# Moving a few waits: splits, loads and sums placed elsewhere in a one-core fp32 decoder layer on Trainium2

## The reference: what is computed

```python
h = rms_norm(x, norm_mix)
proj = h @ w_in + b_in                       # q, k, v of both head groups, gates
o_a = nsa_attention(...)                     # 16 heads: compressed, selected, window branch
o_b = swa_sink_attention(...)                # 16 heads: window of 128, a sink per head
x = x + concatenate([o_a, o_b]) @ w_out      # 2048 x 2048
h = rms_norm(x, norm_ffn)
x = x + (silu(h @ w_gate) * (h @ w_up)) @ w_down     # 2048 -> 5632 -> 2048
return rms_norm(x, norm_final)
```

## Time and profile before

| | value |
|---|---|
| median of three runs | 2010.52 us |
| the profiled execution: its own time | 2010.52 us |
| its span, first to last instruction | 2008.6 us |
| mean granted TensorE clock | 0.999 of full speed |
| PE busy | 1986.3 us (99%) |
| DVE busy | 1635.1 us (81%) |
| ACT busy | 986.1 us (49%) |
| DMA, mean over the span | 153 GB/s |

### The profile page before, as it was taken

One profiled execution on the slowest core, in us unless ns is written; L12 is line 12 of the kernel. 1 busy time (PEld: TensorE's weight loads), 2 busy tenths in 40 slices (PEclk: granted clock), 3 DMA queues, 4 the chain that ended last, 5 costly groups with the idle time before them and its releaser, 6 DMA issues.

```text
span 2008.6 us, 33101 instructions
## 1 busy us (share of the span) xinstructions
PE 1986.3 (99%) x13573; PEld 1793.7 (89%) x13573; DVE 1635.1 (81%) x2308; ACT 986.1 (49%) x1516; POOL 34.8 (2%) x32
## 2 busy tenths in 40 slices
PE   8999999999999999999999999999999999999998
PEld 7888877777679999999999999999999888888886
DVE  6824577878979878988988988988988989889895
ACT  5213367767854575444444444444444433333443
POOL 4000000000000000000000000000000000000002
PEclk9999999999999999999999999999999999999999
DMA  7681322222146352644634634634636764754722
GB/s 274 203 241 44 83 66 62 64 69 59 32 136 210 120 175 85 200 139 147 198 130 154 199 127 157 199 125 147 201 126 219 286 222 157 250 210 168 250 86 84
DMA packets 212439, 306.51 MB, mean 153 GB/s; under 512 B 8960, under 2 KB 147264, under 8 KB 207680
## 3 DMA queue, kind: packets, MB, share of 16 engines
q1 hardware_dynamic: 212256, 304.38, 46.1%
q10 hardware_dynamic: 32, 0.01, 0.0%
HBM read 248.79 MB, written 55.57 MB: 152 GB/s over the span
## 4 chain that ended last, share of the span: by engine, by line
PE 97%; DVE 1%; ACT 1%; issue 1%; DMA 0%; SPq 0%; DVEq 0%; ACTq 0%
PE bank L3109 13%; PE bank L3112 13%; PE bank L3114 13%; PE bank L3164 6%; PE bank L3166 6%; PE bank L3161 6%; PE bank L2651 3%; PE bank L2652 3%; PE bank L2653 3%; PE bank L2822 3%; PE bank L2992 3%; PE bank L2996 3%; PE bank L2994 3%; PE bank L2891 2%; PE bank L2851 2%; PE bank L2972 2%
## 5 line engine op out<-in xcount | busy, mean ns | idle before, releaser
L1497 ACT ACTIVATE w_all<-raw 128x1024 fp32r<-128x1024 f32 x292 | 306.8, 1061 | 310.3 <-PE bank L3166 157.0
L2264 DVE TENSOR_TENSOR w_all<-raw,w_all 128x1024 fp32r<-128x1024 f32 x292 | 352.8, 1219 | 57.2 <-ACT w_all L1497 56.7
L3112 PE MATMUL bank<-x_T,w_all 128*128 128x256 f32 x1344 | 370.9, 276 | 0.0
L3114 PE MATMUL bank<-x_T,w_all 128*128 128x256 f32 x1344 | 370.9, 276 | 0.0
L3109 PE MATMUL bank<-x_T,w_all 128*128 128x256 f32 x1344 | 370.9, 276 | 0.0
L3109 PE MATMUL bank<-x_B,w_all 128*128 128x256 f32 x1008 | 278.3, 276 | 0.0
L3112 PE MATMUL bank<-x_B,w_all 128*128 128x256 f32 x1008 | 278.2, 276 | 0.0
L3114 PE MATMUL bank<-x_B,w_all 128*128 128x256 f32 x1008 | 278.2, 276 | 0.0
L1497 ACT ACTIVATE w_all<-proj_q 128x1024 fp32r<-128x1024 f32 x150 | 158.9, 1061 | 192.8 <-PE bank L3114 125.9
L3112 PEld LDWEIGHTS bank<-x_T,w_all 128*128 128x128 f32 x1344 | 252.3, 188 | 0.0
L3114 PEld LDWEIGHTS bank<-x_T,w_all 128*128 128x128 f32 x1344 | 252.3, 188 | 0.0
(11 more groups left out here) (340 smaller groups left out, 4241.9 us busy)
## 6 DMA issues: line engine op xcount, KB each, us to landing
raw<-in_w_gate SPq DMA_DIRECT2D x39, 1024.0 KB, 5.1
h_scratch<-late SPq DMA_DIRECT2D x70, 512.0 KB, 3.2
raw<-in_w_down SPq DMA_DIRECT2D x50, 512.0 KB, 5.0
proj_q<-in_w_up SPq DMA_DIRECT2D x22, 1024.0 KB, 6.7
raw<-in_w_up SPq DMA_DIRECT2D x22, 1024.0 KB, 8.1
x_B<-h_scratch SPq DMA_DIRECT2D x20, 1024.0 KB, 4.9
raw<-in_w_in SPq DMA_DIRECT2D x16, 1024.0 KB, 10.8
x_T<-h_scratch SPq DMA_DIRECT2D x15, 1024.0 KB, 8.3
```

What stands on the lines that cost most here:

```text
L1497: nc.scalar.activation(piece_hi(p), piece_raw(n, k), ACT.Copy).then_inc(piece_hi_done, 1)
L2264: nc.vector.tensor_tensor(piece_lo(p), piece_raw(n, k), piece_hi(p).bitcast(F32), ALU.subtract).then_inc(piece_lo_done, 1)
L3112: nc.tensor.matmul(dst, wl[:, t, cs], x_hi(x)[:, cols], start=False, stop=False, skip_group_check=True)
L3114: done = nc.tensor.matmul(dst, wh[:, t, cs], x_hi(x)[:, cols], start=False, stop=part == 1 and t == 3, skip_group_check=True)
```

## The change

Five places are written in another order. No arithmetic is added or taken out, and each engine issues the same number of instructions.

1. **ACT, round 6.** The copies of item 4 now come before the bias and the hi part of the minis, as in all other rounds; before, this one round had them behind.
2. **Splits of attention outputs.** `SPLIT_STEP` is one round later for all tiles but tile 7; on DVE `waiting_lo` now belongs to round x and not to x+1. So ACT's hi part moves one round back and DVE's lo part stays in its place, but for tile 7, which goes one round forward.
3. **Loads of w_out.** Unit 2 goes to slot 3 of `raw` and not to `mini_raw`, unit 3 to slot 0. Both wait until all products with V are done, and are issued one behind the other, ahead of B11 and B12. B22 now comes behind the first rows of x and B21 behind the second; before, both came ahead of all rows of x.
4. **DVE before the first piece of group 1.** `s_lo_of(2)` and `out_sum(1, 1)` now come before the lo parts of pieces 0 and 1.
5. **Start of the FFN.** On DVE the lo parts of weight pieces 0 and 1 come before `raise_b11`, and `out_c21(3)` before the lo part of B11. On ACT the hi parts of weight pieces 2 and 3 come before `raise_b("B21")`, and the hi part of each quadrant right behind its raise (before: B12, then B21, both behind the raise of B12). DVE's lo part of B21 comes before that of B12. Some addresses of these tensors are laid out otherwise.

```diff
-X_MADE = {"B11": 0, "B12": 2, "B21": 4, "B22": 6, "T1": 8, "T2": 10, "T3": 12, "T4": 14}
+X_MADE = {"B11": 0, "B21": 2, "B12": 4, "B22": 6, "T1": 8, "T2": 10, "T3": 12, "T4": 14}
...
-SPLIT_STEP = {0: 42, 1: 42, 2: 43, 3: 43, 4: 44, 5: 44, 8: 52, 9: 52, 6: 53, 7: 55}
+SPLIT_STEP = {0: 43, 1: 43, 2: 44, 3: 44, 4: 45, 5: 45, 8: 53, 9: 53, 6: 54, 7: 55}
 SPLIT_ORDER = list(SPLIT_STEP) + list(range(10, KT))
...
         X_SIZE = 2 * HALF_KT * HALF_TOK
-        X_AT = {name: PIECE_AT + 48 for name in x_names}
-        X_AT["B12"] = PIECE_AT + 8
+        X_AT = {name: PIECE_AT + (8 if name == "T3" else 48) for name in x_names}
         with ExitStack() as plain:
...
-        def x_place(name):
-            return "T2" if name == "B12" else name
-
         def x_hi(name):
-            return half_of(xc, x_place(name), 0, X_AT[name])
+            return half_of(xc, name, 0, X_AT[name])
         def x_lo(name):
-            return half_of(xc, x_place(name), 1, X_AT[name])
+            return half_of(xc, name, 1, X_AT[name])
...
-            if n in (0, 2):
+            if n == 0:
                 return mini_raw[:, :, :].rearrange("p s c -> p (s c)")
-            return raw[:, (2, 3)[n // 2], 0:UNIT_COLS * len(OUT_KTS[n])]
+            return raw[:, (OUT0 + n) % RAW, 0:UNIT_COLS * len(OUT_KTS[n])]
...
             load_out(1)
-            sp.wait_ge(lo_done, OUT0 + 1)
+            sp.wait_ge(pv_done, len(PV_RUNS))
             load_out(2)
+            load_out(3)
...
+            sp.wait_ge(lo_done, OUT0 + 1)
             load_out_quad(1, "B11")
             sp.wait_ge(lo_done, OUT0 + 2)
             load_out_quad(1, "B12")
-            sp.wait_ge(pv_done, len(PV_RUNS))
-            load_out(3)
-            load_out_quad(1, "B21")
-            sp.wait_ge(lo_done, OUT0 + 4)
-            load_out_quad(1, "B22")
             sp.wait_ge(s_made, len(S_ORDER))
             sp.wait_ge(oa_lo, len(OUT_AFTER))
             load_rows(0)
+            sp.wait_ge(lo_done, OUT0 + 3)
+            load_out_quad(1, "B22")
             load_rows(1)
+            sp.wait_ge(lo_done, OUT0 + 4)
+            load_out_quad(1, "B21")
             load_rows(2)
...
             for x in range(N_ITEMS + 3):
-                pieces_first = x == EARLY_MINIS
-                if 2 <= x <= N_ITEMS + 1 and not pieces_first:
+                if 2 <= x <= N_ITEMS + 1:
                     copies(x - 2)
                 for run in runs_ended(x - 1):
                     mini_bias(run)
                 for m in minis_of(x + 1):
                     mini_hi_of(m)
-                if pieces_first:
-                    copies(x - 2)
                 if x in STACK_STEP:
...
                       .then_inc(b_raised, 1)
-
-            def b_hi_of(name):
-
-                n = ("B21", "B12", "B22").index(name)
                 for part in range(2):
                     act.wait_ge(b_raised, HALF_KT * n + 4 * part + 4)
                     cols = slice(PIECE * part, PIECE * (part + 1))
-                    dst = x_hi(name)
+                    dst = x_hi("T2" if name == "B12" else name)
                     nc.scalar.activation(dst[:, cols], x_full(name)[:, cols], ACT.Copy)\
...
             row_root_of(1)
-            raise_b("B21")
             piece_hi_of(0, 2)
             piece_hi_of(0, 3)
+            raise_b("B21")
             scale_rows(1)
             raise_b("B12")
-            b_hi_of("B12")
-            b_hi_of("B21")
             raise_b("B22")
-            b_hi_of("B22")
             t_hi_of(1)
...
                     split_lo(OUT0)
-                for t in splits_of(x - 1):
+                for t in splits_of(x):
                     waiting_lo(t)
...
             s_sum_of(3)
+            s_lo_of(2)
+            out_sum(1, 1)
             out_piece_lo(1, 0)
             out_piece_lo(1, 1)
-            out_sum(1, 1)
-            s_lo_of(2)
             for g in range(1, OUT_GROUPS):
...
                 cols = slice(PIECE * part, PIECE * (part + 1))
-                nc.vector.tensor_tensor(x_lo(name)[:, cols], x_full(name)[:, cols],
-                                        x_hi(name)[:, cols].bitcast(F32), ALU.subtract)\
+                where = "T2" if name == "B12" else name
+                nc.vector.tensor_tensor(x_lo(where)[:, cols], x_full(name)[:, cols],
+                                        x_hi(where)[:, cols].bitcast(F32), ALU.subtract)\
                   .then_inc(x_split, 1)
             def b_lo_of(name):
-                n = ("B12", "B21", "B22").index(name)
+                n = ("B21", "B12", "B22").index(name)
                 for part in range(2):
...
             out_c22(3)
+            piece_lo_of(0, 0)
+            piece_lo_of(0, 1)
             raise_b11()
-            piece_lo_of(0, 0)
+            out_c21(3)
             b11_lo_of(0)
-            piece_lo_of(0, 1)
-            out_c21(3)
             b11_lo_of(1)
             row_mean_of(1)
             scale_rows(1)
             piece_lo_of(0, 2)
             piece_lo_of(0, 3)
+            b_lo_of("B21")
             b_lo_of("B12")
-            b_lo_of("B21")
             t_sum(1, "T1", "B12", "B11")
...
                 f = (0, 1, 0, 1)[k // 2]
+                where = "T2" if x == "B12" else x
                 wh, wl = (w.rearrange("p (t c) -> p t c", c=HALF_COLS) for w in (piece_hi(P0[0] + k), piece_lo(P0[0] + k)))
...
                         start = first and half == 0 and k % 2 == 0 and t == 0
-                        nc.tensor.matmul(dst, wh[:, t, cs], x_lo(x)[:, cols], start=start, stop=False,
+                        nc.tensor.matmul(dst, wh[:, t, cs], x_lo(where)[:, cols], start=start, stop=False,
                                          skip_group_check=True)
-                        nc.tensor.matmul(dst, wl[:, t, cs], x_hi(x)[:, cols], start=False, stop=False,
+                        nc.tensor.matmul(dst, wl[:, t, cs], x_hi(where)[:, cols], start=False, stop=False,
                                          skip_group_check=True)
-                        done = nc.tensor.matmul(dst, wh[:, t, cs], x_hi(x)[:, cols], start=False,
+                        done = nc.tensor.matmul(dst, wh[:, t, cs], x_hi(where)[:, cols], start=False,
                                                 stop=last and k % 2 == 1 and t == 3,
```

## The result

| | before | changed |
|---|---|---|
| median | 2010.65 us (6 runs) | 2026.18 us (6 runs, 2023.81 to 2028.7) |
| ratio to before | | 1.0077, 95% interval 1.0066 to 1.0087 |
| profiled execution, span | 2010.52, 2008.6 us | 2025.97, 2024.1 us |
| mean granted TensorE clock | 0.999 | 0.998 |

The change costs 15.5 us. The sign was forecast, the size was not: 8.3 us were expected and 2021.7 was the upper end of the range.

What follows compares the result with a forecast made beforehand. PE was taken as the bound, busy 1986.3 of 2008.6 us. The terms 1.8 + 0.1 + 2.8 + 0 + 2.15 + 0.85 + 0.6 = 8.3 us, added to 2010.5, gave 2018.8; range 2014.0 to 2021.7.

Steps and rivals of the forecast that it cites:

- Part 1: Round 6: keys' split and DVE's copy come later, so PE's transposes near 291 start 1.8 us later.
- Part 2, the wait: Round 54: DVE waits for ACT's late hi part of tile 6, delaying PE's transposes 2.8 us.
- TensorE's clock would stay at 1.0: Whole kernel: no clock loss expected, because gaps of 1.7 us did not lower it before.
- Parts 3 and 4: Output projection: later loads and DVE's new order cost 0 at unit 2, 2.15 at piece 0, 0.85 behind.
- Piece 0: Group 1's start: ready at 608.9 where PE wanted it at 606.81; stall 2.16 us, 0.95 without the late load.
- (b): Rival at the output projection: unit 2 in before 585, DVE never late, B21 in time; 2016.8 us, 20%.
- (c): Rival at round 54: a PE gap between items swallows the wait; 2016.0 us, 12%.
- Unit 2: w_out load: issued at 579.59, landing at 585.3; no PE stall, 0 to 1 us, but DVE 1.98 late.
- the term of 0.85: Output projection: B21 landing late for piece 4, about 0.4 us, and as much again from late DVE; 0 to 1.7.
- Part 5: FFN start: 0.8 us gained at transposes, 0.9 lost at B12's turn, net +0.6 at B12's matmuls.
- (a): Rival: moved waits are covered and only the FFN's start acts; 2009.0 to 2009.7 us, 5%.
- (d): Rival on loads: transfers slower than in rows 4, unit 2 in at 587; 2020 to 2022 us, 18%.

Runs made afterwards that it cites:

- e3: Kernel before with only the attention-output splits' SPLIT_STEP one round later and waiting_lo in the same round: 2015.26 us, ratio 1.0011.
- e1: Changed kernel with one edit, T3's start back at PIECE_AT + 48 and not + 8: 2021.36 us, ratio 1.004.
- e7: Kernel before with the changed w_out and quadrant loads and DVE's new order before group 1's first piece: 2015.54 us, ratio 1.0024.
- e6: Kernel before with only DVE's s_lo_of(2) and out_sum(1, 1) ahead of pieces 0 and 1: 2011.41 us, ratio 1.0007.
- e10: Kernel before with PIECE_AT 32 and not 48, so weight pieces, h and X operands start 16 elements earlier: 2015.14 us, ratio 1.0021.
- e13: Kernel before with only T3's start moved to PIECE_AT + 8: 2014.57 us, ratio 1.0007.
- e4: Kernel before with only ACT's round 6 copies of item 4 ahead of bias and mini_hi: 2012.44 us, ratio 1.0009.
- e8: Kernel before with only the new order at the FFN's start and every X operand at PIECE_AT + 48: 2011.75 us, ratio 1.0009.
- e2: Kernel before with seven X operands of the FFN each at its own start, PIECE_AT + 0 to + 48: 2044.26 us, ratio 1.0151.
- e9: Kernel before with every X operand of the FFN at PIECE_AT + 8: 2042.45 us, ratio 1.0159.
- e11: Kernel before with seven other X operand starts, elements 0 to 128 where all had 96: 2041.3 us, ratio 1.0153.
- e12: Kernel before with DVE's out_c21(3) ahead of B11's lo part and B12 at PIECE_AT + 48: 2040.74 us.
- e14: Kernel before with only DVE's out_c21(3) moved ahead of B11's lo part: 2040.13 us; 8 of 12 runs near 2040.
- e5: Kernel before with only the changed loads of w_out unit 2 and quadrants B22 and B21: 2016.41 us, ratio 1.0017.

## Why the prediction was right and wrong

In this section a measured number stands first and the forecast behind "for".

**Part 1** held: 1.79 for 1.8, with the releaser that was named. That 0.60 of it fell at the mini's matmuls and not at the transposes was a path that the prediction had in its lower bound only.

**Part 2, the wait** held: 2.57 for 2.8; DVE's idle was 4.83 for "about 4". **The sentence that TensorE's clock would stay at 1.0 failed.** It rested on the gaps of 1.67 and less that the kernel before has behind its first microseconds; the replay itself said that this one would be 2.8 to 3.1, and it was not asked what a gap longer than these does. It cost 1.72 us in the profiled execution, and e3 shows it alone; e1 shows that it does not come every time.

**Parts 3 and 4.** Piece 0: 1.84 for 2.15. (The recorded sum for it, (602.66 − 0.60) + 1.23 + 4.4 + 1.2 less 606.81, makes 2.08 and not 2.16, and rivals (b) and (c) together make 2013.95 and not 2013.8; both slips are too small to matter.) Unit 2 was in at 591.2 by ACT's row; shifted back by the 6.1 that the kernel is behind there, that is 585.1, for 585.3 forecast; case (b), in before 585, did not come, if only just. (The Trainium skill's figure, "DMA: Bandwidth & Descriptors", section on the anatomy of one DMA, gave 584.0 as an estimate; the runs are 1.1 later.) B21 landed at 624.5, shifted back 618.4, for 617 to 619. But **the term of 0.85 for it and for a DVE without holes was too small**: 3.6 for 0.85. It was 0.94 at piece 4, then 1.58 up to piece 10, of which 0.76 are the two gaps at 635.94 and 639.56 (DVE late by pieces, as forecast for it), and a further 1.1 up to group 2 without any gap. The 1.9 that are in no gap are pitch: some 118 ns from 633 to 677 us, where the kernel before has that from 606 to 626 and 113 behind. The cause of this stretch stays open. It is not T3's start: from 640 to 660 us PE does 172 matmuls in e1 as in the changed kernel, for 179 in the kernel before. Nor is it any part run alone or parts 3 and 4 together: e7 has 179 there. The operands of this stage lie at the same addresses in all of these; e6 shows that the pitch can change even so, and e10 that it changes with how the operands lie.

**Part 5** held in all its steps: 0.7 won for 0.8, 1.0 lost at B12's turn for 0.9 (0.86 of it a gap), +0.57 net for +0.6 at B12's matmuls. B12, now at + 48 and not + 8, gave 0.29 back in them.

**The step that failed most** is one that the sum does not have: the new `X_AT` was described in the change and priced nowhere. An address was taken for something that costs nothing because no instruction waits for it. (The Trainium skill, "SBUF — State Buffer", section on operand start alignment, says that an operand must start at a multiple of its element size, and that this is about legality and not speed. The runs agree as to legality: all starts ran. As to speed, which the page sets aside, most of the other starts ran slower here.) It was worth 3.6 us (e13), a fourth of the whole. In the trace of before a hint stood ready, though a weak one: B12, the one operand at + 8 there, had its matmuls at a pitch of 116 to 117 ns, and B21 and B22 behind it 113; but B11's, just ahead of it from 737 to 740 us, had 118 at + 48.

From the forecast to the result, by the table: 8.3, and 3.6 for T3's start, 1.7 for the clock and 2.8 for the 0.85 that became 3.6, less 0.9 in small terms (0.3 each at part 2, at piece 0 and at B12's pitch), make 15.5. Added up, the parts run alone give 1.4 (e4) + 4.0 (e3) + 4.6 (e7) + 0.3 (e8) + 3.7 (e13) = 14.0 of 15.5; what is missing is about the size of the slow stretch from 633 to 677 us, which no part alone shows. Of rivals (a), (c) and (d) none came: the waits were not swallowed, and the loads were not slower than in rows 4. The direction came for the reasons given; the range was too narrow because it was made from bounds of waits only.

## What to carry to other kernels

Replaying a new order with old durations gave the waits of parts 1 and 2 and at piece 0 within some 0.3 us, but not those behind the late quadrant (1.7 for 0.85); what it cannot give is a change of the durations themselves. Ask of every edit of an address or a layout which operand it moves against which, look for a tensor in the trace that already lies that way, and compare the start-to-start times of its instructions. When a replay yields a gap on TensorE longer than any in the trace, add the low clock behind it to the upper end (1.7 us behind a gap of 2.9 here, 2.8 behind one of 3.4). And compare traces by how far the same work is behind, not by their waits: half of this loss was in no list of waits.

## What the hardware showed that was not expected

- 48 matmuls of 128x256 take 5.44 us, or 5.6 to 5.8 (113.3 ns from start to start, or a mean of 117 to 120), when only the start of the moving operand is changed, at the same granted clock of 1.00 (e2, e9, e11, e13); with the stationary one moved by as much they keep 5.44 (e10).
- The output projection ran one stretch at 117.8 ns in the kernel before and at 113.3 in e6 (610 to 620 us), with the same addresses and a granted clock of 1.00 in both.
- With the same program and the same addresses, some executions hold the slower pace through the first part of the FFN, some 29 us more; how many depends on the order of work before it, 8 of 116 in the kernel before and 13 of 18 in e12 and e14. None of 27 had it where one product in seven is slow by its address (the changed kernel and e13), but neither had any of the 22 of e5 and e7, whose FFN is the kernel before's, so that may be chance. Why the pace locks in was not found.
- A gap of 2.9 us on TensorE was followed by the lower clock in two profiled executions (the changed kernel, e3) and not in a third (e1); one of 3.44 us was (e5). Behind gaps of 1.69 and less it stayed at 1.00 in the traces of before and of the changed kernel, once it had risen at their start.
- A quadrant of 1024 KB (B21), issued while another one and 1 MB of rows of x were still on their way, landed in 9.2 us, and ACT waited 7.1 us for it while PE's wait was 1.1: the pieces already split were its cover.
